# Low before high at the start of each wide group, and another order of the first attention units, in a two-block transformer kernel

## The reference, cut to what matters

```python
# block 1, layer 0: modulated norm, neighbourhood attention (16 heads), FFN
# block 1, layer 1: modulated norm, QK-norm grouped attention with rotary angles, FFN
s = q @ k.T * scale (+ bias, mask);  p = softmax(s);  o = p @ v
h = h + g1 * (o @ w_o)
h = h + g2 * ((silu(a) * g) @ w_out)          # a, g = ada_norm(h) @ w_in
# block 2, layers 0 and 1: gated convolution and pooling / spatial gating, then
h = h + (silu(conv3(xn @ w_gate)) * (xn @ w_up)) @ w_down
```

## Time and profile before

| | |
|---|---|
| median of three runs | 1519.93 us (1519.59 to 1521.99) |
| the profiled execution's own time | 1521.22 us |
| its span | 1520.0 us |
| TensorE busy | 1504.8 us, 99% |
| VectorE / ScalarE busy | 944.5 us, 62% / 714.6 us, 47% |
| mean granted TensorE clock | 0.999 |

### The profile page before, as it was taken

The page is one execution under the profiler, slowest core; times in us unless marked ns, Lnnn a source line. Parts: engine busy times, 40 slices in busy tenths (PEclk is TensorE's granted clock), DMA queues, the critical chain, the costliest instruction groups (busy, mean ns, idle before and its releaser), DMA issues.

```text
span 1520.0 us, 21592 instructions
## 1 busy us (share of the span) xinstructions
PE 1504.8 (99%) x9007; PEld 1258.6 (83%) x9007; DVE 944.5 (62%) x1245; ACT 714.6 (47%) x1011; POOL 79.0 (5%) x104
## 2 busy tenths in 40 slices
PE   8999999999999999999999999999999999999998
PEld 6777767778888888879778888899888889988887
DVE  6532585553424342476977666679789856779973
ACT  5422585332213222345765545545656546556553
POOL 0220141000000000000010000034000000000000
PEclk9999999999999999999999999999999999999999
DMA  9766425452532232454255555656565554565652
GB/s 361 238 196 213 131 44 177 168 184 93 183 111 83 90 104 90 161 192 131 65 168 192 180 181 186 204 180 214 179 197 178 198 190 153 179 205 170 196 192 83
DMA packets 245298, 252.44 MB, mean 166 GB/s; under 512 B 17758, under 2 KB 238273, under 8 KB 245201
## 3 DMA queue, kind: packets, MB, share of 16 engines
q1 hardware_dynamic: 243648, 248.53, 50.2%
q0 software_dynamic: 944, 1.87, 0.3%
q10 hardware_dynamic: 608, 0.66, 0.1%
HBM read 248.94 MB, written 1.05 MB: 164 GB/s over the span
## 4 chain that ended last, share of the span: by engine, by line
PE 94%; DVE 3%; ACT 2%; DMA 0%; issue 0%; SPq 0%; DVEq 0%; ACTq 0%
PE psum L414 91%; PE psum L1014 3%; DVE wl L400 1%; ACT scr L1055 1%; DMA vtok<-in_ctx 0%; PE psum L985 0%; ACT wh L393 0%; DVE hT L2151 0%; PE psum L583 0%; DVE scr L2097 0%; DVE kl L1610 0%; DVE mix L2111 0%; ACT scr L694 0%; DVE sums L1125 0%; PE psum L2487 0%
## 5 line engine op out<-in xcount | busy, mean ns | idle before, releaser
L400 DVE TENSOR_TENSOR wl<-raw,wh 128x2048 fp32r<-128x2048 f32 (+1 forms) x183 | 413.6, 2262 | 223.6 <-ACT wh L393 223.4
L393 ACT ACTIVATE wh<-raw 128x2048 fp32r<-128x2048 f32 (+1 forms) x183 | 344.3, 1883 | 291.5 <-PE psum L414 285.9
L414 PE MATMUL psum<-x,wh 128*128 128x512 f32 (+1 forms) x1520 | 461.7, 364 | 0.0
L414 PE MATMUL psum<-x,wl 128*128 128x256 f32 x1312 | 367.5, 280 | 0.0
L414 PEld LDWEIGHTS psum<-x,wh 128*128 128x128 f32 x1520 | 271.6, 188 | 48.5 <-issue 1.3
L414 PEld LDWEIGHTS psum<-x,wl 128*128 128x128 f32 x1312 | 248.2, 189 | 0.0
L414 PE MATMUL psum<-xh,wh 128*128 128x512 f32 (+1 forms) x624 | 239.9, 384 | 0.3 <-DVE xl L765 0.3
L414 PE MATMUL psum<-xl,wh 128*128 128x512 f32 (+1 forms) x624 | 236.9, 380 | 0.0
L414 PE MATMUL psum<-xh,wl 128*128 128x512 f32 (+1 forms) x624 | 236.8, 380 | 0.0
L414 PEld LDWEIGHTS psum<-xh,wh 128*128 128x128 f32 x624 | 118.1, 189 | 29.2 <-DVE xl L606 4.3
L414 PEld LDWEIGHTS psum<-xh,wl 128*128 128x128 f32 x624 | 118.2, 189 | 22.1
(11 more groups left out here) (287 smaller groups left out, 2018.0 us busy)
## 6 DMA issues: line engine op xcount, KB each, us to landing
raw<-in_ffn_w_in SPq DMA_DIRECT2D x44, 1024.0 KB, 5.0
pre<-in_ada_w SPq DMA_DIRECT2D x26, 1024.0 KB, 9.7
raw<-in_ada_w SPq DMA_DIRECT2D x22, 1024.0 KB, 6.4
raw<-in_w_ffn_gate SPq DMA_DIRECT2D x22, 1024.0 KB, 5.2
raw<-in_w_ffn_up SPq DMA_DIRECT2D x22, 1024.0 KB, 5.2
raw<-in_w_ffn_down SPq DMA_DIRECT2D x19, 1024.0 KB, 4.8
raw<-in_ffn_w_out SPq DMA_DIRECT2D x16, 1024.0 KB, 4.8
raw<-in_na_w_qkv SPq DMA_DIRECT2D x10, 1024.0 KB, 5.9
```

The lines of the kernel that those rows point to most:

```text
L393: act.e.activation(wh[:, c % NSPL, 0:z], raw[:, p % NRAW, 0:z], ACT.Copy).then_inc(W.hi, 1)
L400: dve.e.tensor_tensor(wl[:, c % NSPL, 0:z], raw[:, p % NRAW, 0:z], wh[:, c % NSPL, 0:z].bitcast(F32), ALU.subtract).then_inc(W.lo, 1)
L414: return pe.e.matmul(o, l, r, start=start, stop=stop, skip_group_check=shared)
```

## The change

In every chunk of a wide group, of its first four pairs the second and the fourth run low, then high; so the matmuls begin high, low, low, high, high, low, low, high. A pair that opens the sum of its bank (k is the first) keeps the plain order: in a `k_outer` group that leaves the fourth pair of the first chunk alone swapped. The other twelve pairs stay.

In the attentions: VectorE in unit 2 of the first attention copies the half of unit 0 before the maxima of unit 2 (`early`); ScalarE's copy of the modulation sums moves from step 2 to step 3, ahead of the exponentials of unit 2; units from 3 on use banks 0 and 4 the other way round, and the wait on the copied sums moves from unit 3 to unit 4. In the second attention ScalarE copies unit 0 before the exponentials of unit 2; TensorE computes the last tile of values at step 1, not 2, and VectorE copies it at step 1; the last query's turning and the reciprocals come behind the maxima of unit 0, and the weight split behind them.

```diff
-                for k, m in [...] if k_outer else [...]:
+                for n, (k, m) in enumerate([...] if k_outer else [...]):
                     ready(k)
                     w = slice(m * P, (m + 1) * P)
-                    mm(o[m], h[:, k - k0, w], x[:, k, :, :]..., k == ks[0], False, True)
-                    last = mm(o[m][:, 0:T], l[:, k - k0, w], x[:, k, 0, :], False, k == ks[-1], True)
+                    first, final = k == ks[0], k == ks[-1]
+                    low_first = n % 2 == 1 and n < turns and not first
+                    for part in "lh" if low_first else "hl":
+                        if part == "h":
+                            last = mm(o[m], h[:, k - k0, w], x[:, k, :, :]..., first, final and low_first, True)
+                        else:
+                            last = mm(o[m][:, 0:T], l[:, k - k0, w], x[:, k, 0, :], False, final and not low_first, True)
...
             for i in range(A_.last):
-                if 0 <= i - 1 < n and not (ahead and i == 3):
+                if i == 3:
+                    between()
+                if 0 <= i - 1 < n:
                     exps(i - 1)
-                if ahead and i == 2:
-                    exps(2)
...
                     dve.wait_ge(S.s, b_.s + i + 1)
                     first(i)
+                    if i == early:
+                        take(i - 2)
                     for h in range(2):
                         b = bank[A_.scores[i] + h][:, :]
                         dve.e.tensor_reduce(...)
+                    behind_max(i)
...
-        SCORES0 = [2, 0, 6] + [4 if i % 2 else 0 for i in range(3, 24)]
+        SCORES0 = [2, 0, 6] + [0 if i % 2 else 4 for i in range(3, 24)]
...
-                elif i == 3:
+                elif i == 4:
                     pe.wait_ge(A.copied, LATE + 1)
                     pe.wait_ge(Q0.act, 20)
...
-            split_for(split_lo, c_qkv1[5])
-            query_turn(3)
-            dve.wait_ge(R1.root, 1)
-            dve.e.reciprocal(rq[:, :], rq[:, :]).then_inc(R1.recip, 1)
...
         def last_values_pe(i):
             if i == 0:
                 values_pe((2,))
-            elif i == 2:
+            elif i == 1:
                 values_pe((3,)).then_inc(W.used, 1)
...
+            def scale(i):
+                if i == 0:
+                    query_turn(3)
+                    dve.wait_ge(R1.root, 1)
+                    dve.e.reciprocal(rq[:, :], rq[:, :]).then_inc(R1.recip, 1)
+                    dve.wait_ge(R1.recip, 1)
             def last_values(i):
-                if i == 2:
+                if i == 0:
+                    split_for(split_lo, c_qkv1[5])
+                elif i == 1:
                     dve.wait_ge(W.used, c_qkv1[5] + 1)
                     dve.e.tensor_copy(v2[:, 2:4, :], two(vbank[1])).then_inc(V1.d, 1)
```

More of the change, by code:

```diff
@@ L450, in tiles_tok, with group_wide @@
             return last
-        def group_wide(o, cs, x, ready, k_outer=False, ks=None):
+        def group_wide(o, cs, x, ready, k_outer=False, ks=None, turns=4):
             total, k0 = sum(weights[c][1] for c in cs), 0
@@ L460, in group_wide @@
                 mine = [k for k in ks if k0 <= k < k0 + nk]
-                for k, m in [(k, m) for k in mine for m in range(2)] if k_outer else [(k, m) for m in range(2) for k in mine]:
+                for n, (k, m) in enumerate([(k, m) for k in mine for m in range(2)] if k_outer else [(k, m) for m in range(2) for k in mine]):
                     ready(k)
                     w = slice(m * P, (m + 1) * P)
-                    mm(o[m], h[:, k - k0, w], x[:, k, :, :].rearrange("p s n -> p (s n)"), k == ks[0], False, True)
-                    last = mm(o[m][:, 0:T], l[:, k - k0, w], x[:, k, 0, :], False, k == ks[-1], True)
+                    first, final = k == ks[0], k == ks[-1]
+                    low_first = n % 2 == 1 and n < turns and not first
+                    for part in "lh" if low_first else "hl":
+                        if part == "h":
+                            last = mm(o[m], h[:, k - k0, w], x[:, k, :, :].rearrange("p s n -> p (s n)"), first, final and low_first, True)
+                        else:
+                            last = mm(o[m][:, 0:T], l[:, k - k0, w], x[:, k, 0, :], False, final and not low_first, True)
                 last.then_inc(W.used, 1)
@@ L1041, in turned, with attention_act @@
             return A_.pt[:, g % 2, h, :, x * P:x * P + P], b[:, :].rearrange("p (c q) -> p c q", q=P)
-        def attention_act(A_, extra, ahead, spread_act):
+        def attention_act(A_, extra, between, spread_act):
             S, b_, n = A_.S, A_.base, A_.n
@@ L1094, in attention_act, with attention_dve @@
                     behind_values(i)
-        def attention_dve(A_, first, middle, prep, spread_act):
+        def attention_dve(A_, first, middle, prep, spread_act, behind_max, early):
             S, b_, n = A_.S, A_.base, A_.n
@@ L1114, in recip, with take @@
                 dve.e.reciprocal(A_.sums[:, 2, at_:at_ + parts, :], A_.sums[:, 1, at_:at_ + parts, :]).then_inc(S.recip, 1)
+            def take(j):
+                g, parts, x, at_ = A_.units[j]
+                if not spread_act:
+                    recip(j)
+                if g >= 2:
+                    dve.wait_ge(S.pv, b_.pv + g - 1)
+                if not spread_act:
+                    dve.wait_ge(S.recip, b_.recip + 2 * j + 1)
+                    dve.e.tensor_copy(A_.wide[:, g % 2, x:x + parts, :, :],
+                                      A_.sums[:, 2, at_:at_ + parts, :].unsqueeze(3).to_broadcast([P, parts, 2, 64])).then_inc(S.recip, 1)
+                if j + 2 > n:
+                    behind_values(j + 2)
+                dve.wait_ge(S.turned, b_.turned + j + 1)
+                to, o = turned(A_, j, 1)
+                dve.e.tensor_copy(to, o).then_inc(S.copied_d, 1)
             for i in range(A_.last):
@@ L1131, in attention_dve @@
                 middle(i)
[L1132 to L1147, removed]
+                if 0 <= i - 2 < n and i != early:
+                    take(i - 2)
                 elif i > n:
@@ L1224, in attention0_act @@
         def attention0_act():
-            def late(i):
-                if i == 2:
-                    ada_copy_act(LATE)
-            attention_act(C0, late, False, True)
+            attention_act(C0, nothing, lambda: ada_copy_act(LATE), True)
         def attention0_dve():
-            attention_dve(C0, biased0, nothing, nothing, True)
+            attention_dve(C0, biased0, nothing, nothing, True, nothing, 2)
         def attention0_pool():
@@ L1555, in qkv1_act, with query_turn @@
             act.e.activation(v2[:, 0:2, :], two(vbank[0]), ACT.Copy).then_inc(V1.a, 1)
+        def query_turn(i):
+            s, q = slot(q_sq[i]), slot(q_cp[i])
+            dve.wait_ge(R1.copy, i + 1)
+            dve.wait_ge(R1.stat, i + 1)
+            dve.e.tensor_tensor(two(s), two(q), cos.unsqueeze(1).to_broadcast([P, 2, T]), ALU.mult).then_inc(R1.cos, 1)
+            if i < 3:
+                query_sin(i)
+                query_sum(i)
         def qkv1_dve():
@@ L1561, in qkv1_dve @@
             normed_low(2, TT, 1, 0, xh3, xl3, 15)
[L1563 to L1570, removed]
             split_for(split_lo, c_qkv1[0])
@@ L1680, in attention1_act @@
             act.wait_ge(R1.recip, 1)
-            attention_act(C1, last_query, True, False)
+            attention_act(C1, last_query, lambda: None, False)
         def attention1_dve():
+            def scale(i):
[4 more added lines that the diff above has]
+                    dve.wait_ge(R1.recip, 1)
             def last_values(i):
-                if i == 2:
+                if i == 0:
+                    split_for(split_lo, c_qkv1[5])
+                elif i == 1:
                     dve.wait_ge(W.used, c_qkv1[5] + 1)
@@ L1697, in last_query @@
                     query_lo(3)
-            dve.wait_ge(R1.recip, 1)
-            attention_dve(C1, nothing, last_values, last_query, False)
+            attention_dve(C1, nothing, last_values, last_query, False, scale, None)
         DN = semaphores(nc, "down", "half res hi lo square sum sum2")
```

## The result

The change makes the kernel slower: 1526.34 us (median of 7 runs, 1524.92 to 1526.52) against 1520.31 us (7 runs, 1518.86 to 1521.99) for the kernel before beside it. The ratio is 1.0031, interval 1.0020 to 1.0041. I had forecast 1517.2 us and a range up to 1522.8. The profiled execution took 1526.45 us, its span is 1525.2 us; the one of before, 1520.0. So of the 6.0 us between the medians, 5.2 are to be found between these two traces.

A forecast was written before the change was run, and what follows sets the result against it. TensorE, busy 99% of the span, was taken as the bound, through the step between matmuls and its few gaps. The terms -2.9 + 0.05 + 0.1 = -2.75 us took the median from 1519.93 to 1517.2 us, range 1515.0 to 1522.8.

The forecast's parts named there:

- What bounds the kernel: Whole kernel: TensorE is busy 99% of the span; only the step between matmul starts and its few gaps can move time.
- Part one: Wide groups: swapped pairs cost nothing by themselves and bring slow stretches from 353.3 to 346.7 ns a pair, -2.9 us.
- What a swap can do is end the slow pattern: Wide groups: two swapped pairs at each chunk's head break the slow three-pair rhythm anew every 16 pairs; gain 2.9 us.
- Rival (b): Chunk heads in wide groups: the swap itself starts the slow rhythm; +7.5 us, 1527.5, with all chunks slow; chance 0.17.
- Part two: First attention: the reorder removes nothing from VectorE's chain, two TensorE gaps become one; +0.05 us, between -0.3 and +0.4.
- Part three: Second attention: VectorE's work is reordered, nothing leaves its chain, new waits come; +0.1 us, between -0.4 and +0.5.
- That is 0.35 in place of 0.22: Second attention: VectorE's waits in us, for the last values (0.2 to 0.3) and the scores of unit 2 (0.1).
- (a): Wide groups: swaps do nothing to the rhythm, slow stretches stay; 1520.1 us; chance 0.19.
- the formula of the Trainium skill: Matmul spacing: columns over 2.4 GHz plus 2.5 ns, so 325 ns a pair in any order; the swaps worth 0.
- (c): Both attentions: the edits win what their gaps show, up to 0.99 + 1.13 us; half gives 1516.1; chance 0.09.
- (d): Half-clock stretch at 694.0 to 697.4 us, costing 1.7 us, may move away or another come: 1515.5 or 1518.9; chance 0.08.
- The range: Whole kernel: 1515.0 to 1522.8 us, the upper end allowing swaps that slow up to 40% of the chunks.

The follow-up runs named there:

- Experiment 1: Kernel before with the swapped pairs alone, attentions as before: 1524.67 us (5 runs), ratio 1.0040.
- experiment 3: Kernel before with two swapped pairs in one chunk only, the fifth group of `up2`: 1523.14 us, one run.
- 5: Kernel before in plain order, plus a one-column matmul ahead of the first group of `o1` and the second of `up1` and `dn1`: 1521.14 us, ratio 1.0003.
- 6: Kernel before plus one-column matmuls ahead of `up2`'s first and `up3`'s fifth group, and one high, high, low, low in `up2`'s fifth: 1522.53 us, one run.
- Experiment 7: Kernel after without swapped pairs, the second attention's last tile of values and its copy back at step 2: 1522.87 us, one run.
- 10: Same code as Experiment 7 (kernel after without swaps, last values back at step 2), now timed: 1521.53 us (11 runs), ratio 1.0004.
- before again: Kernel before, unchanged, profiled once more: 1519.40 us.
- experiment 2: Kernel after with the swaps switched off, both attentions as changed: 1522.28 us (11 runs), ratio 1.0017.
- experiment 9: Kernel before with every second pair of every wide group swapped, timed: 1521.04 us (11 runs), ratio 0.9988.
- Experiment 11: Kernel before with every second pair swapped in all wide groups, plus the new attentions with the last values at step 2: 1519.86 us (11 runs), ratio 0.9988.

## Why the prediction was wrong

**What bounds the kernel: right.** The time moved with the step between matmuls, at an unchanged clock, and nearly nowhere else.

**Part one: wrong, in its sign.** The step that failed is "What a swap can do is end the slow pattern", with "I take the gain of 2.9 us" behind it. Rival (b), the swap itself starts the slow rhythm, came true, at a chance of 0.17. The measured term is +4.9 us, between the two bounds given, -2.9 and +7.5. The upper bound was near but too high, since the swapped order is not at 353.3 ns but at some 352.4: a fast pair loses 5.7 ns and not 6.7. By the starts of the same matmuls in the two traces the stretches that were fast lose 5.8 us (2.75 in `up2` and `dn2`, 1.83 in `up3`, 0.83 from 845 to 912 us, 0.4 in smaller ones), and the others give back 0.9; that is the 4.9. Experiment 1 shows that the swaps do it alone, experiment 3 that two swapped pairs do it to the rest of `up2` and all of `dn2`.

What I had put against (b) was that the slow pattern ended at 1330 us behind a group and a handful of small matmuls, so that it wasn't the state to which TensorE returns. Experiments 5 and 6 show what was wrong in it: there is no state to which it returns. Plain order preserves either rhythm over hundreds of pairs, and an interruption picks one. The observation that spoke for (b), that a group behind a run of 256-column matmuls is slow from its first pair, was the nearer one, but it is no rule either: in experiments 5, 7 and 10 the first group of `up2` behind that same run was fast. That a swapped four acts as such a run in small is argued, not shown. I weighed the price of the new neighbours (120 and 227 ns, near enough) and not what follows them.

**Part two: right.** +0.10 us for +0.05, with the gaps of 0.44 and 0.55 us turned into 0.15 and 0.95. Gaps of TensorE that sum to a microsecond were worth nothing, since VectorE's chain sets the turning of unit 2.

**Part three: right in its mechanism, too small in its size.** The term "That is 0.35 in place of 0.22" came out as 0.64. The wait for the last values was 0.43 and not 0.2 to 0.3, since their matmuls took 3.07 us and not 2.97 (from 729.42 to 732.49) and VectorE was free at 732.17, that for the scores of unit 2 was 0.21 and not 0.1. The stage lost 0.37 us for +0.1, inside the bound of +0.5. Experiment 7 shows the cause: with the copy of the values back at step 2, the stage takes 0.51 us less.

**The other rivals.** (a), swaps that do nothing, is out; its time is missed by 6 us. With it goes, as a guide to this case, the formula of the Trainium skill ("TensorE: Matmul & The Clock Gate", "Back-to-back issue gap"), which the section gives for an isolated matmul and takes from the column count alone. The runs show the same two sizes at 346.5, 348.5 and 353 ns a pair by order and by history. (c) is out by the two stages' times. (d): the half-clock stretch was in seven of the fourteen profiles, each time from 694 or 695 us on, and of two profiles of the same code (before and before again) one has it and one has not, though the run of small matmuls ahead of it is in both. So it belongs to the run and not to the change. It costs 1.5 us where it falls, not the 1.7 of the prediction: the same 72 matmuls take 9.95 us from 690.10 us on in the one and 8.45 from 690.00 in the other. I held it for a property of the program.

**The range.** It ended at 1522.8 because (b) was let in with 40% of the chunks. As the rhythm outlives chunks, with swaps in every chunk a part of them was never likely: all or none was the right pair of cases, and 1527.5 should have counted with its full chance.

**What stays open.** What makes the rhythm in the engine, and what in an entry decides it, no run here shows. The median of experiment 2 lies above its own stages' cost; the likely reason is `up2` at 353 ns in some of its runs (3 us each time, as in 5, 7 and 10), but only one of its runs has a profile, so that is argued and not shown. For the two clumps of runs of experiment 9, 1519.55 to 1519.81 and 1521.04 to 1521.60, the half-clock stretch is the likely reason: their distance of some 1.6 us fits its 1.5, and the mean granted clock was 1.000 or 0.999 in the first and 0.999 or 0.998 in the second. Experiment 11 has the same two clumps, and the one profile of each fits: that of 9 is in the lower clump and has no such stretch, that of 11 in the upper one and has it.

## What to carry to other kernels

Where two matmul sizes alternate back to back, look at the time of three pairs in several stages before anything else: if the same code shows two steps at one clock, an edit of the order can move every pair behind it, and the price is the difference times all of these pairs, not the edited ones. Price a new order by a stretch that has that very order, above all when the old steps are the sum of the parts; here an order of 348.5 ns a pair, which none of its three profiles shows in a slow rhythm, beat one of 346.7 that is often caught in it, by 0.12%. And a gap of the bound engine is only worth what the engine that ends it can give up: the summed gap of 1 us in each attention cost 0.10 and 0.37 us to go after, and even with the values back at their step (experiment 7) the second gave only 0.14.

## What the runs showed of the hardware

- Alternating matmuls of 512 and 256 columns have at least two lasting steps at full clock, 346.7 and 353.3 ns a pair. In single steps the fast one is 230 ns from a high to its low and 116 or 117 from there to the next high, again and again (before, 1110 us); the slow one repeats after three pairs, 232, 241 and 236 ns behind the highs, 118, 120 and 113 behind the lows (before, 950 us). Two swapped pairs took a stretch from the first to the second for 450 pairs; high, high, low, low once did not.
- A pause of 0.14 us can be followed by the fast rhythm where the slow one was the rule (`o1`, 349.7 in place of 356.6 ns over 47.5 pairs, both with a longer first step), or start the slow one (`up3`, 346.2 to 353.6). In the eight profiles with plain order neither rhythm ended without a late matmul, matmuls of another size or an edit.
- Which one a stretch is in changes between runs of one program (`up1`: 353.3 and 346.7 ns over 82 pairs), and with the half-clock stretch of 3.4 us, which costs 1.5, this is the likely reason for runs of the kernel before that lie 6 us apart.
- A run of highs behind a run of lows averages 230 ns over eight, and 227 where there are only highs.
